# Eighteen expert-row dot products per head instead of sixteen, none left for the down stage, and own rows ahead of the last head's extra ones

## What is computed

```python
def peer_ffn(h, wq, keys, u_tab, v_tab):
    def block(hc):
        q = (hc @ wq).reshape(PEER_BLOCK, PEER_HEADS, 2, PEER_DHALF)
        sc = jnp.einsum('thcd,hckd->thck', q, keys).astype(jnp.float32)
        s1, i1 = lax.top_k(sc[:, :, 0], PEER_TOPK)
        s2, i2 = lax.top_k(sc[:, :, 1], PEER_TOPK)
        ...
        top, pos = lax.top_k(cand, PEER_TOPK)
        eidx = jnp.take_along_axis(cidx, pos, axis=-1)
        gate = jax.nn.softmax(top, axis=-1)
        ue = jnp.take(u_tab, eidx, axis=0)
        act = jax.nn.gelu(jnp.einsum('thkd,td->thk', ue, hc).astype(jnp.float32))
        ve = jnp.take(v_tab, eidx, axis=0)
        return jnp.einsum('thk,thkd->td', (gate * act).astype(ve.dtype), ve)
```

## Time and profile before

| what | us |
|---|---|
| median of 3 runs | 3503.8 |
| lowest and highest run | 3500.09 and 3504.2 |
| the profiled execution, own time | 3505.83 |
| its span (first to last instruction) | 3504.1 |
| TensorE busy | 3398.9 (97%) |
| TensorE weight loads busy | 3113.1 (89%) |
| VectorE busy | 2943.3 (84%) |
| ScalarE busy | 1369.3 (39%) |
| GpSimd busy | 958.6 (27%) |

### The profile page before, as it was taken

How to read it: one execution, slowest core, us unless ns; L and a number is a source line. 1 busy time by engine, 2 the same in 40 slices (tenths; PEclk the granted TensorE clock), 3 DMA queues, 4 the chain that set the end, 5 groups by cost and what they waited for, 6 DMA issues and landing times. The chain is left out here.

```text
span 3504.1 us, 67960 instructions
## 1 busy us (share of the span) xinstructions
PE 3398.9 (97%) x27550; PEld 3113.1 (89%) x27550; DVE 2943.3 (84%) x5651; ACT 1369.3 (39%) x2116; POOL 958.6 (27%) x756
## 2 busy tenths in 40 slices
PE   8899899999999999999999989999999999999998
PEld 5678777899999999999997877789999999999997
DVE  8687574899999978888888757489999997888887
ACT  3542353433334443333344234343333444333333
POOL 2000000044453333444510000003445333333352
PEclk9999999999999999999999999999999999999999
DMA  7830432499999999999962043249999999999995
GB/s 233 295 105 28 128 121 67 148 327 344 325 377 311 347 317 348 379 381 377 368 229 84 12 131 111 76 131 334 347 321 376 313 349 317 365 378 384 375 365 203
DMA packets 392169, 922.19 MB, mean 263 GB/s; under 512 B 33968, under 2 KB 211248, under 8 KB 385072
## 3 DMA queue, kind: packets, MB, share of 16 engines
q1 hardware_dynamic: 298672, 582.20, 48.6%
q0 software_dynamic: 93184, 335.65, 25.4%
HBM read 802.51 MB, written 113.05 MB: 261 GB/s over the span
## 5 line engine op out<-in xcount | busy, mean ns | idle before, releaser
L2570 POOL DMA_INDIRECT row<-in_peer_u_rows,row_at x320 | 424.4, 1326 | 654.2 <-DVE row L2908 574.3
L228 PE MATMUL peer_ps<-peer_h_high,tile_high 128*128 128x352 f32 (+1 forms) x1504 | 496.4, 330 | 6.3 <-DVE tile_low L221 6.2
L229 PE MATMUL peer_ps<-peer_h_low,tile_high 128*128 128x352 f32 (+1 forms) x1504 | 492.1, 327 | 0.0
L230 PE MATMUL peer_ps<-peer_h_high,tile_low 128*128 128x352 f32 (+1 forms) x1504 | 491.5, 327 | 0.0
L221 DVE TENSOR_TENSOR tile_low<-peer_tile,tile_high 128x1024 fp32r<-128x1024 f32 x362 | 439.6, 1215 | 27.2 <-ACT tile_high L216 26.9
L228 PE MATMUL peer_ps<-gate_high,tile_high 128*128 128x352 f32 x1360 | 441.0, 324 | 2.4 <-DVE tile_low L221 2.3
L230 PE MATMUL peer_ps<-gate_high,tile_low 128*128 128x352 f32 x1360 | 441.5, 325 | 0.0
L229 PE MATMUL peer_ps<-gate_low,tile_high 128*128 128x352 f32 x1360 | 439.6, 323 | 0.0
L216 ACT ACTIVATE tile_high<-peer_tile 128x1024 fp32r<-128x1024 f32 x362 | 379.8, 1050 | 80.6 <-DMA peer_tile<-in_peer_u 75.6
L216 ACT ACTIVATE gate_high<-weighed 128x352 fp32r<-128x352 f32 x256 | 127.8, 499 | 619.0 <-DMA peer_tile<-in_peer_v 301.8
L2908 DVE SCALAR_TENSOR_TENSOR row<-row,h_own 128x1024 f32<-128x1024 f32 x256 | 308.7, 1218 | 14.7 <-DMA row<-in_peer_u_rows,row_at 14.6
(11 more groups left out here) (569 smaller groups left out, 8042.7 us busy)
## 6 DMA issues: line engine op xcount, KB each, us to landing
peer_tile<-in_peer_u SPq DMA_DIRECT2D x256, 512.0 KB, 6.3
peer_tile<-in_peer_v SPq DMA_DIRECT2D x256, 512.0 KB, 6.2
gates<-gates_out SPq DMA_DIRECT2D x44, 1024.0 KB, 9.1
gates_in<-gates SPq DMA_DIRECT2D x32, 1408.0 KB, 10.0
acts<-up_act SPq DMA_DIRECT2D x220, 176.0 KB, 6.9
act_in<-acts SPq DMA_DIRECT2D x220, 176.0 KB, 6.4
in_w<-in_w_in SPq DMA_DIRECT2D x32, 512.0 KB, 3.6
peer_tile<-in_peer_wq SPq DMA_DIRECT2D x32, 512.0 KB, 4.5
```

Of the source, the lines that this page charges most:

```text
L228: pe.matmul(out, wh, mh, start=first, stop=False)
L229: pe.matmul(out, wh, ml, start=False, stop=False)
L230: return pe.matmul(out, wl, mh, start=False, stop=last)
L2570: pool.indirect_dma_start(row_of(n)[:, :], None, table, bass.IndirectOffsetOnAxis(ap=row_at[:, row_col(n):row_col(n) + 1], axis=0)) \
```

## The change

1. `ROWS_BY_HEAD` goes from 16 to 18, so that the seven searches with rows hold 126 dot products instead of 112. The tables of row numbers for the gate placement and the part gathers move with it.
2. The last head's row order begins with three own rows of earlier heads (`own + 3`) instead of its own extra rows.
3. In the groups the first three each do one row (`max(min(g + 1, 3), ...)`); the total over the groups stays 16. One round of parts moves from group 4 to group 5, and the making of its weights, with the GELU ahead of it, from group 3 to 4.
4. The last up tiles do 1.2 rows each, 14 in all instead of 18. With this all 160 are done before the down stage.
5. `DOTS_UNTIL` = 2: no dot product stands in the down stage, the GELU comes ahead of the rounding of its fourth tile, and the V rows begin at the fifth tile instead of the eleventh: 128 rows over 120 tiles instead of 114.

```diff
--- before.py
+++ after.py
@@ -2282,8 +2282,8 @@
 PARTS = 4
 EX_ROUNDS = PH * EX_COLS // PARTS
 BATCH = PH // 2
-ROWS_BY_HEAD, ROWS_BY_GROUP, ROWS_BY_TILE = 16, 0.75, 1.5
-DOTS_UNTIL = 8
+ROWS_BY_HEAD, ROWS_BY_GROUP, ROWS_BY_TILE = 18, 0.75, 1.2
+DOTS_UNTIL = 2
 ROWS_END = NKEY - 4
 PAIRS = ((0, 1, 16), (1, 2, 8), (3, 4, 4), (7, 8, 2), (15, 1, 1))
 GAPS = 29
@@ -2310,7 +2310,7 @@
 
     order, own = [], 0
     for hd in range(PH):
-        first = min(hd * TOPK, own + ROWS_BY_HEAD // 2) if hd + 1 < PH else own
+        first = min(hd * TOPK, own + ROWS_BY_HEAD // 2) if hd + 1 < PH else own + 3
         until = min((hd + 1) * TOPK, own + ROWS_BY_HEAD - EX_COLS) if hd + 1 < PH else OWN
         order += [*range(own, first), *(OWN + hd * EX_COLS + j for j in range(EX_COLS)), *range(first, until)]
         own = until
@@ -2322,11 +2322,11 @@
 PLACE_AT = [min(max(n - 3, hd * ROWS_BY_HEAD), next(j for j in range(ROWS) if ROW_ORDER[j] // TOPK == hd)) if hd > 1 else
             min(n, next(j for j in range(ROWS) if ROW_ORDER[j] // TOPK == hd)) for hd, n in enumerate(EXTRA_FROM)]
 DOTTED_EXTRA = [ROW_ORDER.index(OWN + BATCH * (b + 1) * EX_COLS - 1) + 1 for b in range(2)]
-PART_GATES_AT = (71, 119)
-PART_GATHER_AT = {48: 0, 89: 1, 100: 2, 108: 3, 122: 4, 125: 5, 128: 6, 131: 7}
-PART_STATIONS_AT = ({5: (0, 1), 6: (2,), 7: (3,)}, (3, 6, 9, 13), ((4,), (5,), (6,), (7,)))
+PART_GATES_AT = (79, 133)
+PART_GATHER_AT = {54: 0, 99: 1, 112: 2, 120: 3, 136: 4, 139: 5, 142: 6, 145: 7}
+PART_STATIONS_AT = ({5: (0, 1), 6: (2,), 7: (3,)}, (4, 6, 9, 13), ((4,), (5,), (6,), (7,)))
 PART_SUMS_AT = {(6, 2): 0, (6, 9): 1, (7, 4): 2}
-PART_SUMS_IN_SPREAD = {0: 3, 4: 4, 8: 5, 11: 6, 15: 7}
+PART_SUMS_IN_SPREAD = {0: 3, 5: 4, 8: 5, 11: 6, 15: 7}
 
 
 def row_col(n):
@@ -3121,7 +3121,7 @@
                 if g in PART_STATIONS_AT[1]:
                     for r in PART_STATIONS_AT[2][PART_STATIONS_AT[1].index(g)]:
                         make_stations(r)
-                rows(searched_rows + 4 + int(ROWS_BY_GROUP * (g + 1)))
+                rows(searched_rows + 4 + max(min(g + 1, 3), int(ROWS_BY_GROUP * (g + 1))))
             for m in range(done[0], UPS):
                 lows(1)
                 rows(searched_rows + 4 + int(ROWS_BY_GROUP * GROUPS) + int(ROWS_BY_TILE * (m + 1 - GROUP_AT[GROUPS])))
```

## The result

The changed kernel takes 3544.3 us (median of 4 runs, 3543.86 to 3552.98), the kernel before 3504.0 beside it (4 runs): ratio 1.0121, 95% interval 1.0102 to 1.0141. It is 40 us slower; the forecast of 3511.5 us had the sign and missed four fifths of the size, and the range ended at 3522. The profiled execution of the changed kernel is the longest of its four runs, 8.7 us over their median, so its stages are a little too long; a second profile, of run f0_after, stands beside it.

The account below looks back on a forecast made before the run. Searches bound by matched VectorE and TensorE, down stage by TensorE: 20.8 - 5.4 - 5.7 - 2.0 = +7.7 us, 3513.5 us for the profiled execution, 3511.5 us for the median. Range 3503 to 3522 us.

Parts of the forecast that it names:

- Dot products into the searches: Searches of both layers: two more dot products per search lengthen VectorE-bound windows, +20.8 us, bounds +18.8 and +27.4.
- With them VectorE has 320.0 us of work for 310.9 us: Heads 2 to 7, layer 1: twelve added dot products, 13.7 us, on 306.29 us busy; growth 9.1 us if gaps fill.
- 0.7 us per layer for the last head's transfers: Last search: two more rows at 384 GB/s make transfers take 53.9 us where VectorE needs 53.2.
- The two uncovered dot products: Head 1's start and behind the last found indices: covered by VectorE's idle time, costed at nothing, otherwise 1.14 us each.
- Rows late behind the part gathers: Rival, searches: rows behind four part gathers land late, up to 4.1 us each, 16.4 us over both layers; chance 0.09.
- The last head's extra rows: Behind the last search: own rows gathered during placement cover TensorE's wait, -5.4 us over both layers, bounds -6.0 and 0.
- landing like the fourth of now (1074.46, about 9.5 us behind its issue): Behind the last search: the extra row, now fourth, is used at 1070.6, the low made some 3.7 us earlier.
- the bubble stays: Rival, behind the last search: placement, not row order, holds the bridge, so 5.4 us aren't won, 3517 us; chance 0.06.
- The last up tiles: Last up tiles: 14 dot products instead of 18 remove waits for rows, -5.7 us over both layers, bounds -7.1 and 0.
- The down stage: Down stage: removed dot products give nothing, some TensorE waits are taken back, -2.0 us together, bounds -5.8 and +2.
- Transfers bound the down stage: Rival, down stage: it goes by bytes, fewer U rows save 13.8 us per layer, giving 3486 us; chance 0.06.
- The marks named ahead: Changed profile: search windows 320 to 321 us, VectorE over 99%, low waits 8 us or more, down stage change under 3.

Follow-up runs that it names:

- f0_after: The changed kernel run again without alteration, against the kernel before: 3541.6 us, ratio 1.0110.
- f3: Changed kernel with every U row gathered by the first head's indices, so no gather waits for a search, and later placements: 3523.9 us, ratio 1.0060.
- g4: Changed kernel with U rows gathered as in f3 and second V rows placed as in g1: 3511.5 us, ratio 1.0020.
- e3: Kernel before with only parts 2 and 3 of the change (own rows first, matching group rows): 3499.9 us, ratio 0.9990.
- g1: Changed kernel with one V row per down tile and a second always in tiles 10, 18, 26, ...: 3528.9 us, ratio 1.0071.
- h2: g1 with one more VectorE operation of 1.2 us (a low made twice) in every eighth down tile: 3549.8 us, ratio 1.0165.
- g2: Kernel before with only its second V rows moved, to down tiles 13, 21, 29, ...: 3562.3 us, ratio 1.0159.
- f1: Changed kernel with V rows still from the fifth down tile but at 1.12 per tile instead of 1.07: 3582.3 us, ratio 1.0222.

## Why the prediction was wrong
- **Dot products into the searches, forecast +20.8 us.** The step "With them VectorE has 320.0 us of work for 310.9 us" held to 0.2 us, and f3 and g4 show windows of 319 to 322 us once rows are known. What failed is the end of the sum, where nothing but VectorE's work was to lengthen these windows. The change doesn't only add two rows per search; it takes rows out of the reserve between what is gathered and what is used (18 used per head where 20 are made known, instead of 16). No view of before shows this, since there nothing waits; the row numbers do, set beside the places where GpSimd's loop stops. Measured +33.5 us in this execution, of which 11.8 are VectorE's waits for rows. The 0.7 us per layer for the last head's transfers at 384 GB/s had no ground either: over its last search f3 (1011.92 to 1065.01) moves 410 GB/s, and VectorE is busy 53.06 of those 53.09 us.
- **The two uncovered dot products, costed at nothing.** The one at the bridge was free. That at head 1's start was not: it is wanted at once, its gather is issued only at 690.67, behind the placement, and VectorE waits 4.9 us for it; tiles 12 to 24 get 1.9 us longer in layer 1 and none in layer 2. "Covered by idle time" holds for the operation, not for the wait that stands ahead of it.
- **Rows late behind the part gathers, chance 0.09.** Half of this rival came true: about 5 of the 11.8 us of waits stand behind part gathers, with up to 1.4 us each and not the 4.1 that the rival took as its most. The other half stands behind the finds, which no case had. Its chance was set low on the median landing of 7.7 us; the first rows behind four part gathers take 7.6 to 10.1 us from issue to use (row 54: 852.10 to 861.32), and those are the rows that count.
- **The last head's extra rows, forecast -5.4 us.** In after nothing is won (28.6 and 27.7 us for 28.3 and 27.8). The own rows came in time, as said. The step that failed is "landing like the fourth of now (1074.46, about 9.5 us behind its issue)". The changed kernel has it so, GpSimd first, then VectorE and TensorE:

```profile
1073.52 0.59 POOL L2537 DMA_DIRECT2D row_at<-extra_at  x1 [10.81 <-DVE row_at L2985]
...
1079.12 0.94 POOL L2570 DMA_INDIRECT row<-in_peer_u_rows,row_at  x1 [0.30 <-issue]
...
1086.44 1.23 DVE L2908 SCALAR_TENSOR_TENSOR row<-row,h_own 128x1024 f32<-128x1024 f32 x1 [0.33 <-DMA row<-in_peer_u_rows,row_at]
1090.35 1.23 DVE L2908 SCALAR_TENSOR_TENSOR row<-row,h_extra 128x1024 f32<-128x1024 f32 x1 [2.68 <-DMA row<-in_peer_u_rows,row_at]
1093.29 1.22 DVE L221 TENSOR_TENSOR peer_tile_low<-peer_tile,peer_tile_high 128x1024 fp32r<-128x1024 f32 x1 [1.70 <-ACT gate_row L2805]
...
1094.57 0.66 PE L228 MATMUL peer_ps<-peer_h_high,peer_tile_high 128*128 128x352 f32 x1 [2.88 <-DVE peer_tile_low L221]
```

  The extra row took 11.2 us from issue (1079.12) to use (1090.35), at the end of a search in which the DMA share stood at 1.01. But it didn't come last. Behind it the low waits 1.70 us more, for ScalarE's `gate_row` (in the program the low stands behind a wait for these copies, `flip_taken`), and ScalarE is late with them because the `high` ahead of them waited for a tile load. ScalarE:

```profile
1090.66 1.06 ACT L216 ACTIVATE tile_high<-peer_tile 128x1024 fp32r<-128x1024 f32 x1 [2.98 <-DMA peer_tile<-in_peer_u]
...
1092.97 0.28 ACT L2805 ACTIVATE gate_row<-peer_ps 128x96 f32<-128x96 f32 x1
```

  So by this trace the low would have started no sooner with the row in time. It is the same in layer 2 and in both layers of f0_after: the low's last wait, 1.7 to 2.7 us, is for `gate_row`, behind a wait of ScalarE of 2.0 to 2.9 us for a tile load. The sum named only rows and took TensorE itself for what is late next; the path over ScalarE is what it missed. (Its 3.7 us should also read 3.9, 1074.46 - 1070.6.) With 16 rows per head the part gives 1.4 and 1.9 us (e3), and where all rows are known it gives 2.7 and 2.2 (g4, 25.6 us), close to the 2.9 and 2.5 forecast; there no tile load is late at that place. The rival "the bubble stays" had the outcome, not the cause: in after and f0 no own row was waited for by more than 0.6 us.
- **The last up tiles, forecast -5.7 us.** Right: 46.5 us in both layers, twelve steps of 3.88 us, 2.4 and 3.6 us less. In layer 1 TensorE waits for nothing there, though VectorE still waits 1.4 us for rows, over the 0.5 named as the mark.
- **The down stage, forecast -2.0 us, bounds -5.8 and +2.** Wrong in sign and far off in size: +18 us in the profiled execution, and the placing of the double tiles is worth 14 us of the median (g1). The step was "that is 0.03 MB less per tile", a mean. V rows come in whole rows, one tile in 15 has two, and this tile wanders through all eight places against the slab load, three of them bad by the table above. The bounds were built from TensorE's waits in the kernel before, 2.1 and 0.2 us, which only tell that its double tiles lay well. Its VectorE share of 86% there says nothing of how late a tile may be.
- **Transfers bound the down stage, chance 0.06.** Against it now stand 10 fewer dot products, a lower rate and a longer stage. (It was priced at 380 GB/s, which no row has; at the 361 of the earlier trace rows it would be 14.5 us per layer.)
- **The marks named ahead.** TensorE's waits for lows in the searches are over 8 us per layer, as said (12.2 and 11.6). The windows are 327.4 and 325.6 us and not 320 to 321, VectorE is busy 98% of them and not over 99%, the wait behind the last search is 2.9 us and not under 0.5, and the down stage is 8.4 and 9.8 us longer where it was to change by under 3. Of the marks of error, "VectorE waits for rows in the searches" came true.

## What to carry to other kernels
Where a consumer uses up what a producer makes known, count the reserve at each hand-over, not only the time of the added work: with 16 rows used per head 5 or 6 were in hand at every find, with 18 it was 3 to 5 at the first ones, and knowing all rows ahead was worth 9 us per layer. Where a schedule spreads n things over m turns by integer division, look at which turns get two, and where these fall against the next larger periodic transfer; keep the two periods equal (here 8 and 8) and place the doubles behind the transfer. An engine that is busy 85% of a stage (420.1 of 494.7 us in g1) may still have no room in one turn out of eight: h2 put 1.2 us there and lost 21 us.

## What the runs showed of the hardware that was not expected
- One slab load of 1408 KB in the same queue holds up the 512 KB load behind it: 13.1 us from issue to use in g2, 10.0 in g1. Over layer 1's down stage the raw loads land after 3.6 / 6.0 / 9.6 us (least, median, longest) in g1 and after 3.4 / 6.8 / 14.8 in g2:

```profile
DMA to landing us min/median/max: 3.6/6.0/9.6
...
DMA to landing us min/median/max: 3.4/6.8/14.8
```

- Sixteen VectorE operations of 1.2 us per layer, in a stage where VectorE is idle for some 75 us (420.1 of 494.7 us busy in g1), cost 21 us in h2, more than half of their own sum of 38 us over both layers.
- The same 128 V rows per layer, with the double tiles at 5 modulo 8 instead of 2 and 3 and no other change, cost 60 us in 3502 (g2); f1, with doubles at 4 and 5 modulo 8, is 53 us over g1.
